# Routed experts dealt in 64-slot units, two experts sharing a tile by column halves, and rows summed once at the end

## What is computed

```python
scores = jax.nn.sigmoid(jnp.einsum('nd,de->ne', t, w_router).astype(jnp.float32))
# ... the best 4 of 8 groups, in them the best TOP_K = 8 of 64 experts for each token
w = jnp.take_along_axis(scores, idx, axis=1)
w = w / jnp.sum(w, axis=-1, keepdims=True) * ROUTED_SCALE
...
a = jax.nn.silu(t @ wg) * (t @ wu)          # 1024 -> 256, per expert
return acc + g[:, None] * (a @ wd), None    # 256 -> 1024, gate g
...
return (routed + shared).reshape(B, L, D)
```

## Time and profile before

| | |
|---|---|
| three runs | 2030.07 us median, 2028.19 to 2030.41 |
| the profiled execution | 2028.67 us, its span 2026.8 us |
| PE busy | 1890.4 us, 93% of the span |
| DVE, ACT, POOL busy | 645.5, 445.8, 411.0 us |
| moved by DMA | 419.35 MB |

### The profile page before, as it was taken

How to read it: one execution, slowest core, us unless ns; L and a number is a source line. 1 busy time by engine, 2 the same in 40 slices (tenths; PEclk the granted TensorE clock), 3 DMA queues, 4 the chain that set the end, 5 groups by cost and what they waited for, 6 DMA issues and landing times.

```text
span 2026.8 us, 25917 instructions
## 1 busy us (share of the span) xinstructions
PE 1890.4 (93%) x8348; PEld 1188.2 (59%) x8348; DVE 645.5 (32%) x1571; ACT 445.8 (22%) x946; POOL 411.0 (20%) x661
## 2 busy tenths in 40 slices
PE   5999789989998899999979899999999999999994
PEld 2844467567767668888766444444444444444443
DVE  1215841694269550001266311111111111111114
ACT  1204521452144430000021111111111111111112
POOL 0003420353034100000002322222222222222220
PEclk8999989999999999999978899999999999999997
DMA  9123332111210553210114699999999999999952
GB/s 391 42 83 124 136 126 83 42 45 45 83 43 4 214 204 125 94 72 9 42 41 182 253 371 365 373 367 368 372 363 373 355 381 359 375 367 368 373 165 95
DMA packets 56948, 419.35 MB, mean 207 GB/s; under 512 B 6289, under 2 KB 10001, under 8 KB 31145
## 3 DMA queue, kind: packets, MB, share of 16 engines
q1 hardware_dynamic: 33689, 339.19, 42.0%
q0 software_dynamic: 21456, 78.10, 14.7%
q10 hardware_dynamic: 1728, 1.05, 0.2%
HBM read 362.70 MB, written 55.61 MB: 206 GB/s over the span
## 4 chain that ended last, share of the span: by engine, by line
PE 80%; DVE 9%; ACT 5%; DMA 3%; issue 1%; POOL 1%; SPq 0%; POOLq 0%; DVEq 0%; ACTq 0%
PE ps L1039 25%; PE ps L1061 12%; PE ps L901 10%; PE ps L862 9%; PE ps L847 7%; PE ps L1030 3%; PE ps L933 3%; DVE work L1439 2%; ACT work L585 2%; PE ps L818 2%; ACT work L587 2%; DVE work L1428 1%; DMA Xb<-xT 1%; PE ps L1000 1%; DMA st_out<-work 1%
## 5 line engine op out<-in xcount | busy, mean ns | idle before, releaser
L1039 PE MATMUL ps<-W,work 128*128 128x512 f32 x1168 | 515.2, 594 | 1.6 <-ACT work L1223 1.2
L1039 PEld LDWEIGHTS ps<-W,work 128*128 128x128 f32 x1168 | 216.9, 191 | 247.7 <-issue 247.7
L1061 PE MATMUL ps<-work 128*128 128x512 f32 x576 | 259.1, 592 | 0.0
L1749 DVE SCALAR_TENSOR_TENSOR work<-ps,work 128x256 f32<-128x256 f32 x73 | 35.3, 484 | 515.1 <-ACT work L1229 515.1
L862 PE MATMUL ps<-Hb,W 128*128 128x260 f32 x768 | 172.8, 389 | 0.1
L1061 PEld LDWEIGHTS ps<-work 128*128 128x128 f32 x576 | 103.8, 190 | 103.3 <-issue 103.3
L862 PEld LDWEIGHTS ps<-Hb,W 128*128 128x128 f32 x768 | 148.4, 194 | 23.9 <-ACT work L1123 0.5
L1258 POOL TENSOR_TENSOR work<-work 128x128 f32<-128x128 f32 x168 | 82.8, 525 | 381.2 <-ACT work L587 380.8
L1759 DVE COPY work<-ps 128x512 f32<-128x512 f32 x144 | 99.7, 692 | 178.8 <-DMA ffrows<-work 91.9
L1328 POOL DMA_INDIRECT ffrows<-work x72 | 115.7, 1607 | 195.8 <-DVE work L1759 122.4
L847 PE MATMUL ps<-W,Hb 128*128 128x512 f32 (+1 forms) x320 | 138.4, 592 | 0.0
(11 more groups left out here) (255 smaller groups left out, 2232.1 us busy)
## 6 DMA issues: line engine op xcount, KB each, us to landing
W<-wexp SPq DMA_DIRECT2D x74, 2048.0 KB, 8.7
work<-wexp SPq DMA_DIRECT2D x73, 1024.0 KB, 8.0
W<-wq SPq DMA_DIRECT2D x36, 2048.0 KB, 8.0
work<-st_in SPq DMA_DIRECT2D x8, 1024.0 KB, 9.3
st_out<-work SPq DMA_DIRECT2D x8, 1024.0 KB, 7.5
Xb<-xT SPq DMA_DIRECT2D x2, 2080.0 KB, 18.2
h2rows<-work SPq DMA_DIRECT2D x5, 512.0 KB, 2.6
yT<-Xb SPq DMA_DIRECT2D x2, 1040.0 KB, 5.2
```

The costliest lines, as they stand in the source:

```text
L1039: mm = pe.matmul(ps[:, k % 2, :], xe[:, k % 2, c, :], GU[:, k % 4, c, :], start=(c == 0), stop=(c == KC - 1))
L1061: mm = pe.matmul(ps[:, 4 + hf, :], aT[:, k % 2, f, :], WD[:, k, f, hf * 512:(hf + 1) * 512], start=(f == 0), stop=(f == 1))
```

## The change

- **Units.** An expert gets one 128-slot tile for each full pair of 64-slot units and, if a unit is left over, a half tile. Counted out as above there are 28 pairs and 43 left-over units. The loop has passes of two tiles: the tile of kind A (`k == 0`) holds one expert, the tile of kind B (`k == 1`) two column halves of 64 slots, each with its own expert's weights. 43 halves fill 22 tiles; with 28 pairs this is 50 tiles, 25 passes. Pairs beyond the 25th are put in a B tile as two halves of the same expert. Each pass loads the weights of three experts.
- **Slots.** Three weight slots in place of four: one for A, two for B; each is loaded again only once its own tile has used it. The gather buffers `xg` are two in place of four, and the gather ahead of tile t's scatter is that of t+2, not t+3.
- **Rows.** Tile outputs are not gated and not accumulated: each choice has a row of its own in `yrows` (4160 rows) and is written there once by a plain indirect DMA. After the loop, SP loads for each token its eight rows (17 MB in all), and DVE adds them with their gates onto the shared expert's rows, which now stay in SBUF (`rows_`). The tokens' blocks are taken in the order 4, 0, 1, 2, 3 (block 4 has 8 tokens).
- **Tables.** One table of 68 tiles (the choice number) in place of three of 96.
- **Merge order.** The list has one decode item after each of the first 15 products, in place of two at every third.

The diff, cut to its core:

```diff
-        for k in range(12):
+        for k in range(15):
             ORDER.append(("P", k))
-            for _ in range(2 if k % 3 == 0 else 1):
-                ORDER.append(decode.pop(0))
-        ORDER += [("N1", 0), ("P", 12), ("S", 0), ("N2", 0)] + [("P", k) for k in range(13, 4 * len(MERGE))]
+            ORDER.append(decode.pop(0))
+        ORDER += [decode.pop(0), ("N1", 0), ("P", 15), ("S", 0), ("N2", 0)] + [("P", k) for k in range(16, 4 * len(MERGE))]
...
-        xg = [view(work, 8192, D), view(work, 9216, D), view(OB, 0, D), view(OB, D, D)]
+        xg = [view(work, 8192, D), view(work, 9216, D)]
...
             with sp.Fori(1, nq) as i:
-                for k in range(4):
-                    gate(sp, "sp", s_hh, i * 4 + (k + 2))
-                    load_tile(i * 4 + (k + 1), (k + 1) % 4, "gu", s_gu)
-                    gate(sp, "sp", s_y, i * 8 + (2 * k + 2))
-                    load_tile(i * 4 + k, k, "dn", s_dn)
-            gate(sp, "sp", s_add, nq * 64 + 32)
-            for t in range(TT):
+                gate(sp, "sp", s_hh, i * 2 + 3)
+                load_expert(i, 0, "gu", s_gu)
+                gate(sp, "sp", s_hh, i * 2 + 4)
+                for h in range(2):
+                    load_expert(i * 2 + (NLIST + h), 1 + h, "gu", s_gu)
+                gate(sp, "sp", s_y, i * 4 + 6)
+                load_expert(i, 0, "dn", s_dn)
+                gate(sp, "sp", s_y, i * 4 + 8)
+                for h in range(2):
+                    load_expert(i * 2 + (NLIST + h), 1 + h, "dn", s_dn)
...
+            for m, t in enumerate(TAIL):
                 n = min(P, NT - t * P)
-                sp.dma_start(work[0:n, t * D:(t + 1) * D], ffrows[t * P:t * P + n, :]).then_inc(s_f1[t], 16)
+                since(sp, s_acc, m - 2)
+                for h in range(2):
+                    sp.dma_start(picked[m % 3][0:n, h * 4096:(h + 1) * 4096],
+                                 yrows[t * P * TOPK:(t * P + n) * TOPK, :].rearrange("(t k) d -> t (k d)", k=TOPK)
+                                 [:, h * 4096:(h + 1) * 4096]).then_inc(s_f1[m % 3 * 2 + h], 16)
...
+            def parts(k):
+
+                return [(slice(0, TS), 0)] if k == 0 else [(slice(0, UNIT), 1), (slice(UNIT, TS), 2)]
...
                 for c in range(KC):
-                    mm = pe.matmul(ps[:, k % 2, :], xe[:, k % 2, c, :], GU[:, k % 4, c, :],
-                                   start=(c == 0), stop=(c == KC - 1))
+                    for at, slot in parts(k):
+                        mm = pe.matmul(ps[at, k, :], xe[:, k, c, at], GU[:, slot, c, :], start=(c == 0), stop=(c == KC - 1))
...
             with pool.Fori(0, nq) as i:
-                for k in range(4):
-                    gather(i * 4 + (k + 3), (k + 3) % 4, i * 8 + (2 * k + 4))
-                    gate(pool, "pool", s_add, i * 64 + (16 * k + 32))
-                    pool.tensor_copy(ida[:, k:k + 1], idx_i[:, bass.ds(i * 4 + k, 1)]).then_inc(s_ic, 1)
-                    gate(pool, "pool", s_yc, i * 8 + (2 * k + 4))
-                    gate(pool, "pool", s_ic, i * 8 + (2 * k + 5))
-                    pool.indirect_dma_start(out=ffrows, out_offset=bass.IndirectOffsetOnAxis(ap=ida[0:TS, k:k + 1], axis=0),
-                                            in_=yb[0:TS, k % 2, :], in_offset=None, compute_op=ALU.add).then_inc(s_add, 16)
+                for k in range(2):
+                    gather(i * 2 + (k + 2), k, i * 4 + (2 * k + 3))
+                    gate(pool, "pool", s_add, i * 32 + (16 * k + 32))
+                    pool.tensor_copy(ida[:, k:k + 1], idy_i[:, bass.ds(i * 2 + k, 1)]).then_inc(s_ic, 1)
+                    gate(pool, "pool", s_yc, i * 4 + (2 * k + 4))
+                    gate(pool, "pool", s_ic, i * 4 + (2 * k + 4))
+                    pool.indirect_dma_start(out=yrows, out_offset=bass.IndirectOffsetOnAxis(ap=ida[0:TS, k:k + 1], axis=0),
+                                            in_=yb[0:TS, k, :], in_offset=None).then_inc(s_add, 16)
...
+            def total(m):
+                t = TAIL[m]
                 rows = min(P, NT - t * P)
+                row = rows_[t][0:rows, :]
+                for k in range(TOPK):
+                    if k % 4 == 0:
+                        dve.wait_ge(s_f1[m % 3 * 2 + k // 4], 16 * (m // 3 + 1))
+                    if k or m:
+                        dve.wait_ge(s_fs, TOPK * m + k)
+                    dve.scalar_tensor_tensor(out=row, in0=picked[m % 3][0:rows, k * D:(k + 1) * D], scalar=gk[0:rows, t, k:k + 1],
+                                             in1=row, op0=ALU.mult, op1=ALU.add).then_inc(s_fs, 1)
...
+            for m in range(TT):
+                total(m)
+                if m:
+                    residual(m - 1)
+            residual(TT - 1)
```

More of the change, by code:

```diff
@@ L292, in decoder_step @@
         slotk = view(OB, 2520, TT * 8, "p (t k) -> p t k", t=TT)
[L293 to L297, removed]
+        pairs = view(OB, 2560, NE)
+        odd = view(OB, 2624, NE)
+        thr = view(OB, 2688, NE)
+        shift = view(OB, 2752, NE)
+        rounded = view(OB, 2816, NE)
+        idxt = view(OB, 2880, MAXT + 4)
+        pad = view(OB, 960, MAXT + 4)
+        less = view(OB, 1040, MAXT + 4)
+        less_i = view(OB, 1120, MAXT + 4).bitcast(I32)
+        order = view(OB, 2960, 2 * NE, "p (a e) -> p a e", a=2)
+        before = view(OB, 3088, 2 * NE, "p (a e) -> p a e", a=2)
+        assert 2880 + MAXT + 4 <= 2960 and 3088 + 2 * NE <= R0
         gsum = view(tiny, 32, TT)
-        ecol = view(tiny, 37, 1)
-        erow = tiny[0:1, 64:64 + MAXT + 4]
+        ecol = view(tiny, 37, 2)
+        n_pair, n_all, n_two, two_end, skip = (view(tiny, 40 + k, 1) for k in range(5))
+        over, quadn = view(tiny, 46, 1), view(tiny, 48, 1)
+        erow = tiny[0:1, 64:64 + 2 * NLIST]
         ui = ints[:, 0:TT * 8].bitcast(U32).rearrange("p (t k) -> p t k", t=TT)
@@ L330, in decoder_step @@
         ida = view(work, 16216, 4).bitcast(I32)
-        gcol = view(work, 16220, 4)
+        rows_ = [view(OA, t * D, D) for t in range(4)] + [view(Hb, 0, D)]
+        picked = [work[:, 0:8192], W[:, 0:8192], W[:, 8192:16384]]
+        TAIL = [4, 0, 1, 2, 3]
         LSQ = view(work, 0, KC * NT, "p (c t) -> p c t", c=KC)
@@ L1330, in _ @@
-            for p in range(4):
-                gate(pool, "pool", s_ga[p], nq * 16 + (16 if p < 3 else 0))
+                for k in range(2):
+                    gather(i * 2 + (k + 2), k, i * 4 + (2 * k + 3))
[5 more added lines that the diff above has]
+                                            in_=yb[0:TS, k, :], in_offset=None).then_inc(s_add, 16)
@@ L1334, in _ @@
+            for k in range(2):
+                gate(pool, "pool", s_ga[k], nq * 16 + 16)
         @block.vector
@@ L1668, in _ @@
             dve.wait_ge(s_rp, 1)
[L1669 removed]
+            step(dve.tensor_scalar(rounded, ps[:, 3, 0:NE], float(UNIT - 1), None, ALU.add))
             settled()
[L1671 removed]
+            step(dve.tensor_copy(whole, rounded))
             settled()
[L1673 to L1675 removed]
@@ new lines, in _ @@
+            step(dve.tensor_scalar(order[:, 1, :], order[:, 1, :], order[:, 0, NE - 1:NE], None, ALU.add))
+            settled()
+            step(dve.tensor_scalar(before[:, 0, :], order[:, 0, :], R("part2"), None, ALU.is_le))
+            settled()
+            step(dve.tensor_reduce(ecol[:, 0:1], before[:, 0, :], AX, ALU.add))
+            settled()
+            step(dve.tensor_scalar(before, order, two_end, None, ALU.is_le))
+            settled()
+            step(dve.tensor_reduce(ecol[:, 1:2], before.rearrange("p a e -> p (a e)"), AX, ALU.add))
@@ new lines, in _ @@
+                rank = ps[0:r, 4, t.start * NE:t.stop * NE].rearrange("p (t e) -> p t e", t=n)
+                step(dve.tensor_tensor(pos[0:r, t, :], rank, wide(thr), ALU.subtract))
+                settled()
+                step(dve.scalar_tensor_tensor(out=tmp[0:r, t, :], in0=pos[0:r, t, :], scalar=0.0, in1=wide(shift),
+                                              op0=ALU.is_ge, op1=ALU.mult))
+                settled()
+                step(dve.tensor_tensor(pos[0:r, t, :], pos[0:r, t, :], wide(order[:, 0, :]), ALU.add))
@@ L1697, in _, with pick @@
+                settled()
+                step(dve.tensor_tensor(pos[0:r, t, :], pos[0:r, t, :], tmp[0:r, t, :], ALU.add))
             settled()
-            for dst, src in ((posk, pos), (gk, gates)):
+            def pick(dst, src):
                 step(dve.tensor_tensor(prod, oh, src.rearrange("p t (a e) -> p t a e", a=1).broadcast_to([P, TT, TOPK, NE]), ALU.mult))
@@ L1702, in _ @@
                 settled()
+            pick(posk, pos)
             step(dve.tensor_copy(posi, posk.rearrange("p t k -> p (t k)")))
@@ L1740, in _ @@
+            step(dve.tensor_copy(idy_i, less))
+            settled()
+            dve.tensor_copy(idx_i, idxt).then_inc(s_T, 1)
+            pick(gk, gates)
+            dve.sem_inc(s_gk8, 1)
             dve.sem_inc(s_a, 2)
```

314 lines of the change are left out of this document (170 added, 144 removed).

## The result

The changed kernel takes 2265.2 us (median of 4 runs, 2263.8 to 2267.3), the one before 2030.2: a ratio of 1.116, 95% interval [1.114, 1.118]. It is 235 us slower; the prediction had 2144 with 2010 to 2235 around it, so the sign and the place were right and the size was half of what came. Spans, by which the stages can be added: 2265.4 against 2026.8 us.

The account below looks back on a forecast made before the run. PE was taken to bound the kernel before, a gather ring the changed loop. Profiled 2028.7 us + 79 (loop) + 48 (behind it) - 4 (before it) - 9 (merge) = 2142.7, stated as 2144 for the median; range 2010 to 2235.

Parts of the forecast that it names:

- What bounds the kernel now: Expert loop before the change: PE is the bound at 11.4 us a tile, with DMA close under it.
- the gather's new place closes a ring: Expert loop: scatter, gather, landing, `turn`, down projection, next scatter; 8.6 us plus landing time a tile, 36 us a pass.
- The halves overlap: B tile's matmuls: two column halves run side by side, 11.4 us a tile; the rival without overlap had 0.07.
- The turns from one width to the other: PE's changes between full and half-width matmuls in the loop: nothing in the sum; by the drain rule 16 us.
- the landing of a gather behind a B tile: Expert loop: the gather waits for the weights' backlog, landing at 14.8 us after the B tile's down projection ends.
- D: The end of a tile's down projection, where the next transposes start; times in the loop are counted from it.
- The clock, charged once: Expert loop: half clock behind the long wait adds 1.7 us to `turn` and down projection, giving 36 us a pass.
- the landing behind the A tile: Expert loop: the gather behind an A tile lands at 29.6 us of the pass, the next down projection ending at 34.2.
- The tail: Behind the loop: last write, loads, 40 sums of 1.25 us on DVE, residuals and the rest, 99 us in sum, +48.
- The merge: Merge before the layer norm: more products between the decode items fill most of PE's waits, -9 us (-5 to -15).
- Tables: Before the loop: smaller and fewer tables save 5 us, longer index arithmetic costs one, -4 us (0 to -7).
- DMA bounds the loop and the gathers come in time: Expert loop, faster rival: gathers land in about 4.9 us, 27 to 28.5 us a pass, total 1918 to 1956; chance 0.13.

## Why the prediction missed

- **What bounds the kernel now, and that the gather's new place closes a ring:** right. The gather alone, put late in the kernel before, costs 360 us; put early in the changed kernel, it gives 260 back. The chain of the changed kernel runs through the steps named.
- **The halves overlap:** right, 7.09 against 7.03 us in `gate_up`, and 3.65 against 3.60 in the down projection at the full clock. The turns from one width to the other, for which the sum had nothing, do cost something: 0.15 us each where PE is never idle, four a pass, and together they are all of the 0.6 us by which the pass without a third of the weights exceeds 22.8. That agrees with the drain between tiling modes which the Trainium skill has in TensorEngine Tiling (Array Packing), Key Properties, and with the 0.16 us that the prediction took for it. In the changed kernel only one of the four, ahead of the B tile's down projection, lies on the ring: some 4 us of the loop, an estimate from these rows.
- **The step that failed is the landing of a gather behind a B tile.** The prediction had "a request that finds a backlog waits for it", from the earlier trace rows, and so a landing at D + 14.8, 10.8 us after the issue. It landed at D + 18.6, 14.76 after the issue. In the rows of before the queue of the weights had run nearly empty by the time POOL's data moved: 1.8 MB went through it between the scatter's issue and 1514.9, and the next load was issued only at 1516.72, so waiting and taking turns look alike there. The queues are served in turns of one packet, and behind a B tile 4.2 MB of weights in rows of up to 16 KB stand in the other. Nor did the queue end there: the B tile's next gate and up weights, two loads of 2 MB that SP issues once `gate_up` ends at 1522.6, joined the turns while the gather crawled, where the prediction had them wait behind it. That is +3.8 us a pass. I took the state of the DMA system from a stretch with a short queue and extended it to one with more than twice as much.
- **The clock, charged once:** half right. Behind the long wait it was at 0.50, as said. Behind the short wait, 2.79 us, it was too in the pass shown, and the down projection there took 5.16 us, where it takes 3.61 at the full clock; the prediction had named this as "once more for the short wait at most". Over the loop the second charge comes in every pass, behind the short wait or as a longer stretch behind the long one.
- Together, for the pass shown: +3.8 for the landing; +1.9 for the short wait (`turn` and down projection 6.22 us, 1508.96 to 1515.18, for a forecast 4.31, of which 0.15 is the change of width); -0.3 for the landing behind the A tile (9.9 us behind that tile's D, forecast 10.2); -0.2 for the clock behind the long wait (5.79 for 6.0). That makes 5.2, and 41.2 against 36 is 5.2. In the middle of the loop a pass is 4.9 us over the forecast, over the whole loop 4.3, which is the gap between +79 and +187.
- **The tail:** right, +52 for +48. 40 sums at a pace of 1.32 us, not 1.25, make 3 of the 4. The loads came within 8% of being felt, as the halved sums showed.
- **The merge:** right in kind, -6.5 for -9, all of it the order. **Tables:** wrong by 6 us. The tables themselves gained 3, not 5: their blocks took 7.9 and 9.6 us in turn, and in the longer ones, where POOL's pace leaves PE idle between the tables, L1036 took 5.35 us instead of 3.65, with a granted clock of 0.67 over it. The index arithmetic from the last table to the first gather took 8.0 us instead of 3.4, where the prediction had one microsecond for it, and the layer norm's matmuls 1.5 more; the pieces between gave 1.3 back. **Before the merge** the changed kernel is 4 us later, but that isn't shown to be a cost of the change: the kernels that have its code up to there reach the first product anywhere from 681.6 to 685.8 us, those with the code of before from 680.4 to 682.6.
- **The rival "DMA bounds the loop and the gathers come in time"** was given 1918 to 1956 us if a gather could land in 4.9 us. The volume was right, 26.9 us a pass and 1931 in all, once two orders of issue were put right; the landing never had to be short, it had to be asked for a tile earlier.

What stays open: q0 starts to move data 5 us after the scatter's issue behind a B tile (1517.02, nothing on q0 till 1522) and 3 us after it behind an A tile (1541.84, till past 1544). Turns by packet don't explain why there is no turn in those first microseconds. It is not that the weights ahead must be through, as some of the down weights still moved beside q0 from 1522 to 1524; no run took this apart.

## What to carry to other kernels

When a change takes away a buffer or a step of lookahead, write down the ring that this may close, from one wait through the in-order queues back to it, and give its length beside those of the bounds that the change is about: 25 passes times the ring cost more here than all 22 saved tiles brought. Price a small transfer beside large ones by its own number of packets and the length of the packets in the other queue, not by the bytes ahead of it. And when the load of a slot stands in an in-order queue behind waits for other slots, compare when the slot came free with when the load was issued; here 8 us between them cost 3 us a pass.

## What the runs showed of the hardware

- Two DMA queues take turns by packet: 252 to 251 packets in 10 us beside rows of 16 KB, 280 to 276 in 5 us beside rows of 4 KB. A gather of 4 KB rows landed in 14.8 us beside loads with rows of 16 KB, in 8.1 beside rows of 4 KB, and in 5.7 (median) where the engines were at 257 GB/s.
- TensorE's clock was at 0.50 behind waits of 2.79 (in 15 of 24 passes) and of 11.49 us, and was at 0.99 over 600 us where matmuls of constants filled them.
- Two column halves with different weights ran side by side in fp32: 32 matmuls of 64 columns in 7.09 us, 16 of 128 in 7.03.
- A change between full and half width cost 0.15 us with PE never idle: four a pass, 23.4 us instead of 22.8.
- The core's DMA engines kept 425 GB/s over 400 us with three kinds of transfers in two queues.
